# Query weights of heads 2 and 3 placed in two row buffers; expert rows start in the third buffer

## The chip, the cores and the metric

One core of one Trainium2 chip runs the whole kernel. The metric is the device time of one execution in microseconds (us), as the median of several runs.

## The reference, cut to what matters

Two transformer blocks over 256 tokens of width 1024, all in float32. What matters here is the PEER layer at the end of the first block: each token picks 16 of 16384 experts for each of 8 heads, and adds their gated outputs.

```python
def peer(h, w_pq, sub_keys, u_emb, v_emb):
    q = (h @ w_pq).reshape(B, S, PEER_HEADS, 2, PEER_DHALF)          # 8 heads x 2 x 128
    sc = jnp.einsum("bshcd,hcnd->bshcn", q, sub_keys)                # 128 keys per half
    s_top, i_top = lax.top_k(sc, PEER_TOPK)
    cand = s_top[..., 0, :, None] + s_top[..., 1, None, :]           # 16 x 16 candidates
    best, pos = lax.top_k(cand, PEER_TOPK)
    expert_idx = ...                                                 # 16 experts per head and token
    gate = jax.nn.softmax(best, axis=-1)
    # per token: a = gelu(u_emb[expert_idx] . h);  out = sum(gate * a * v_emb[expert_idx])
```

With 128 tokens on the partitions, one "row" of the kernel is one rank of one head for 128 tokens: 128 experts' u and v (1024 + 1024 floats each), fetched from DRAM by index. There are 2 token tiles x 8 heads x 16 ranks = 256 rows of 1 MiB (1.05 MB).

## The kernel before, in words

The kernel is written engine by engine, with hand-placed waits on semaphores; the order of the instructions in each engine's block is the order in which it runs them.

**The weight ring.** All dense weights but one piece come as a stream of chunks of up to 2 MiB (`chunk_list`, L82) through a ring of three slots, loaded by SyncE (L690 to L698). Chunk n goes to slot n mod 3 and waits until the chunk three before it has been used for the last time (`LAST_USE`, L222, or the end of its last part). The order around the change is `attno` 0, 1, `convout` 0, 1, `wout` 0, 1, then the query weights `pq` 0, 1 and 3 (each holds two heads: `pq` 1 is heads 2 and 3), then `va`, `cqkv` 0, `cqkv` 1, `qa`, `ka`. So `pq` 0 waits for `convout` 1, `pq` 1 for `wout` 0, `pq` 3 for `wout` 1, `va` for the last use of `pq` 0 (fill `("pqt", 1, 1)`), `cqkv` 0 for that of `pq` 1 (fill `("pq", 3)`) and `cqkv` 1 for that of `pq` 3 (fill `("pq", 7)`). The weights of heads 4 and 5 (`EARLY_QUERY`, L79) lie elsewhere, loaded in four pieces behind `wout` 0 (L703).

**Fills.** TensorE writes each result into one of six PSUM banks in one fixed order (`fill_list`, L183); `bank_filled` counts them, and other engines wait for a count.

**The start of the expert layer.** TensorE multiplies by `wout`, normalises and turns token tile 0 and computes the first head's query and scores (`first_query_and_scores`, L1138). VectorE selects the first 16 experts in two halves (`first_selection`, L2190, first half signalled at L2218). Then come token tile 1, the queries of heads 0 and 1 (`tile_query`, `tile_scores`) and, on VectorE, the whole selection of head 1 before the first row.

**The row loop**, 256 rows, each passed through four engines:

- GpSimd issues the indirect load of row n (L740 to L753) into row buffer n mod 8 of `gath`, which lies over the first 16384 columns of `pool`, 2048 columns a buffer. Buffers 0 to 3 lie below the split `wout` weights; from row 4 on (`ROWS_BELOW_WEIGHTS`, L167) it first waits for the fill `("wout", 1, 1)`. Row 8 and every 16th row wait for the selection; from row 8 on, row n also waits until row n - 8 has been used by TensorE (`wait_spent`, L624).
- VectorE makes the dot product of the u half with the token (`dot`, L2235, L2242), and between the dots the selection of the head after next (`select_step`).
- ScalarE makes gelu, gate and a 128x128 diagonal, two rows at a time (L1654 to L1671), four diagonals deep.
- TensorE multiplies the diagonal by the v half (two matmuls of 512 columns, L1221) into two PSUM banks of their own.

**Queries inside the row loop.** Heads 2 to 7 have their query (`pq`, 16 accumulated products of 256 columns for both token tiles, L800) and scores (`sc`, L1201) placed ahead of certain rows of TensorE's order by `QUERY_SLOTS` (L163). ScalarE copies each out after the diagonal four rows later (`QUERY_COPY_AFTER`, L166).

After the row loop come the rest of the second block's projections, attentions and feed-forward layers, which the change leaves as they are but for the ring slots that their chunks lie in.

Of the kernel before, what the change touches and what calls it, by code (L numbers as in the profile page):

```python
# [25 lines left out]
D = 1024  # L26
# [50 lines left out]


EARLY_QUERY = 2  # L79


def chunk_list():  # L82
    out = [(("glu", i), 4096) for i in range(4)] + [(("q1", i), 4096) for i in range(2)] + [(("kv1", 0), 2048)]
    out += [(("gate", i), 4096) for i in range(4)]
    out += [(("attno", i), 4096) for i in range(2)] + [(("convout", i), 4096) for i in range(2)]
    out += [(("wout", i), 4096) for i in range(2)]
    out += [(("pq", i), 4096) for i in range(4) if i != EARLY_QUERY]
    out += [(("va", 0), 4096), (("cqkv", 0), 4096), (("cqkv", 1), 4096), (("qa", 0), 4096), (("ka", 0), 4096),
            (("kpe_uq", 0), 3328), (("uq_ukv", 0), 3584), (("evout", 0), 4096), (("evout", 1), 4096)]
    for layer in range(2):  # L90
        if layer:
            out += [(("uz", 0), 4096), (("vz", 0), 4096), (("qd", 0), 4096), (("kd", 0), 4096), (("vd", 0), 4096),
                    (("ws", 0), 1024), (("odout", 0), 4096), (("odout", 1), 4096)]
        out += [(("gu%d" % layer, i), 4096) for i in range(KF // 2)]
        out += [(("down%d" % layer, i), min(4, KF - 4 * i) * D) for i in range(-(-KF // 4))]
    return out
# [61 lines left out]
def fm_fills(name, chunks=1):  # L158
# [1 line left out]

QUERY_SLOTS = {0: ("pq", 2), 2: ("sc", 2), 8: ("pq", 3), 14: ("sc", 3), 19: ("pq", 4), 25: ("sc", 4),  # L163
               30: ("pq", 5), 36: ("sc", 5), 42: ("pq", 6), 48: ("sc", 6), 54: ("pq", 7), 60: ("sc", 7)}
QUERY_LAG = 4
QUERY_COPY_AFTER = {n + (QUERY_LAG if n else 0): fill for n, fill in QUERY_SLOTS.items()}  # L166
ROWS_BELOW_WEIGHTS = 4  # L167
SELECT_FIRST_AT = (7, 8, 9, 10, 11, 12, 13, 14, 15)
TOKEN_CHUNKS = (("va", 0), ("cqkv", 0), ("cqkv", 1))
NORM_SLOT = 15  # L170
# [150 lines left out]
        self.scale, self.table, self.sinks, self.column = scale, table, sinks, column  # L321


def build(nc, stream, early_query, consts, t5const, params, rows, keys_in, late_rows, x_in, positions, t5_in, rpb_in, uv, out):
    with ExitStack() as ctx:
        def sb(name, shape, dt=F32):
            return ctx.enter_context(nc.sbuf_tensor(name, shape, dt))
# [1 line left out]
        def sem(name):  # L329
            return ctx.enter_context(nc.semaphore(name))  # L330
# [113 lines left out]
        qpT = view(att, 5120, 2, 2, S)  # L444
        keys = tab[:, :, :].rearrange("p h j -> p (h j)")[:, 0:2048].rearrange("p (m n) -> p m n", n=NKEYS)
        gath = view(pool, 0, NROWS, 2 * D)
        scores = view(att, 0, NT, 2 * PH * NKEYS)
        cand = att[:, 4096:4096 + TOPK * TOPK]
        first_cand = att[:, 1024:1024 + TOPK * TOPK]
# [57 lines left out]
        row_landed = sem("row_landed")  # L507
        keys_landed = sem("keys_landed")
        early_query_landed = sem("early_query_landed")
        pos_landed = sem("pos_landed")  # L510
        t5_landed = sem("t5_landed")
        rpb_landed = sem("rpb_landed")
# [171 lines left out]
        @block.sync  # L684
        def _(sp):
            for t in range(NT):
                sp.dma_start(x[:, t, :], x_in[P * t:P * t + P, :]).then_inc(x_landed[t], 16)
            sp.dma_start(cst[:, :], consts).then_inc(const_landed, 16)
            sp.dma_start(par[:, :], params).then_inc(param_landed, 16)
            for n, (name, width) in enumerate(CHUNKS):  # L690
                if n >= NSLOT:
                    before = CHUNKS[n - NSLOT][0]
                    if before in LAST_PART:
                        wait_part_used(sp, *LAST_PART[before])
                    else:
                        sp.wait_ge(bank_filled, FILL_NO[last_use(before)] + 1)
                src = stream[CHUNK_AT[n]:CHUNK_AT[n + 1]].rearrange("(p w) -> p w", p=P)
                sp.dma_start(ring[:, n % NSLOT, 0:width], src).then_inc(chunk_landed[n % NSLOT], 16)  # L698
                if name == ("wout", 0):
                    sp.wait_ge(bank_filled, FILL_NO["attno", 1, 1] + 1)  # L700
                    sp.wait_ge(t5_stored, 16)
                    sp.wait_ge(rpb_stored, 16)
                    for c, piece in enumerate(query_pieces):  # L703
                        sp.dma_start(piece, early_query[:, 1024 * c:1024 * c + 1024].rearrange("p (k n) -> p k n", k=2)
                                     ).then_inc(early_query_landed, 16)
            for t in range(NT):
                sp.wait_ge(out_ready, t + 1)
                sp.dma_start(out[P * t:P * t + P, :], xn[:, t, :]).then_inc(out_stored, 16)
            sp.wait_ge(out_stored, 16 * NT)
# [3 lines left out]
        def _(gp):  # L713
# [26 lines left out]
            for n in range(NT * SLOTS):  # L740
                if n == ROWS_BELOW_WEIGHTS:
                    gp.wait_ge(bank_filled, FILL_NO["wout", 1, 1] + 1)
                if n == 0:
                    gp.wait_ge(first_ranks, 1)
                elif n == TOPK // 2:
                    gp.wait_ge(selected, 1)
                elif n % TOPK == 0:
                    gp.wait_ge(selected, n // TOPK + 1)
                if n >= NROWS:
                    wait_spent(gp, n - NROWS)  # L750
                gp.indirect_dma_start(out=gath[:, n % NROWS, :], out_offset=None, in_=uv,  # L751
                                      in_offset=bass.IndirectOffsetOnAxis(ap=experts[:, n:n + 1], axis=0)
                                      ).then_inc(row_landed_in[n % NROWS], 16)  # L753

# [24 lines left out]
        def _(pe):  # L779
# [404 lines left out]
            def query(kind, head):  # L1184
                dst = begin((kind, head))
                if kind == "pq":
                    if head // 2 == EARLY_QUERY:
                        pe.wait_ge(early_query_landed, 16 * len(query_pieces))
                        w = [query_pieces[k // 2][:, k % 2, :] for k in range(KD)]
                    else:  # L1190
                        chunk = wait_chunk(pe, ("pq", head // 2))[:, 0:4096].rearrange("p (k n) -> p k n", k=KD)
                        w = [chunk[:, k, :] for k in range(KD)]
                    for j in range(2):
                        c = 2 * P * (head % 2) + P * j
                        last = accumulate(dst[:, S * j:S * j + S], [(w[k][:, c:c + P], hT[:, k, :]) for k in range(KD)])
                else:
                    wait_emptied(pe, ("pq", head))
                    for t in range(NT):
                        for c in range(2):
                            at = 2 * NKEYS * t + NKEYS * c  # L1200
                            last = nc.tensor.matmul(dst[:, at:at + NKEYS], qpT[:, head % 2, c, tile128(t)],  # L1201
                                                    keys[:, 2 * head + c, :], start=True, stop=True)
                last.then_inc(bank_filled, 1)

            for t in range(NT):
                if t:
                    pe.wait_ge(sums_added, 2 * t)
                for k in range(SLOTS):
                    n = SLOTS * t + k
                    if n in QUERY_SLOTS:  # L1210
                        query(*QUERY_SLOTS[n])
                    if t and k == NORM_SLOT:
                        tile_transposes("mix0", 0, xn[:, 0, :])
                    if t and k in TOKEN_SLOTS:
                        if k == TOKEN_SLOTS[0]:
                            wait_tile("mix0", 0)
                        name, i = TOKEN_CHUNKS[TOKEN_SLOTS.index(k)]
                        token_chunk(name, i, 0)
                    pe.wait_ge(diag_ready, n + 1)
                    for half in range(2):  # L1220
                        last = nc.tensor.matmul(psum[:, RB + half, :], diag[:, n % NDIAG, :],  # L1221
                                                gath[:, n % NROWS, D + 512 * half:D + 512 * half + 512],
                                                start=k == 0, stop=k == SLOTS - 1)
                        if k == SLOTS - 1:
                            last.then_inc(sums_done, 1)
                    if k < SLOTS - 1:
                        last.then_inc(row_spent, 1)
# [512 lines left out]
        def _(dve):  # L1740
# [494 lines left out]
            def dot(n):  # L2235
# [2 lines left out]
                if k == 0 and pair >= 4:  # L2238
                    dve.wait_ge(acts_ready, pair - 3)
                dve.wait_ge(row_landed_in[n % NROWS], 16 * (n // NROWS + 1))  # L2240
                row_u = gath[:, n % NROWS, 0:D]
                ins = V.tensor_tensor_reduce(out=row_u, in0=row_u, in1=xn[:, n // SLOTS, :], scale=1.0,  # L2242
                                             scalar=0.0, op0=ALU.mult, op1=ALU.add,
                                             accum_out=dots[:, pair % 4, k:k + 1])
# [261 lines left out]
```

## Time and profile before

| | us |
|---|---|
| median of 3 runs | 1607.2 |
| lowest, highest | 1601.48, 1609.42 |
| the profiled execution's own time | 1604.03 |
| its span, first to last instruction | 1602.1 |
| busy: TensorE | 1447.7 |
| busy: VectorE | 1017.3 |
| busy: ScalarE | 646.3 |
| busy: GpSimd | 312.3 |
| GpSimd's first and last row issued at | 266.8, 927.7 |

The profile gives the busy time of each engine, the share of the span and rate of the 16 DMA engines, the chain of work that ended last (followed back from the last instruction through what released each step), and every instruction with what ended the idle time before it. TensorE's busy time is modelled and overlaps: its sum in a stretch is no proof that it was at its peak. An issue of a DMA is listed at the time at which the engine gave it out, and not at its landing.

### The profile page before, as it was taken

The page shows a single profiled execution, that of the slowest core. Times are in us where ns is not written, and L with a number is a line of the kernel's source. Part 1 is how long each engine was busy: PE and PEld are TensorE (multiplying, and loading weights), DVE is VectorE, ACT ScalarE, POOL GpSimd, SP SyncE. Part 2 cuts the span into 40 slices and gives each one's busy share as a digit, 9 for nine tenths or more (in the row PEclk, how much of TensorE's full clock was granted, in tenths as well). Part 3 has the DMA queues.
Part 4 walks back from the last instruction along what each step waited for, and adds up shares of the span by engine and source line. Part 5 has one row for each costly group of instructions (what it writes and reads, how often), then busy time and mean ns, then how long its engine had stood idle before and what let it go on. Part 6 is the DMA issues. An engine that isn't in the chain of part 4 may idle for free.

```text
span 1602.1 us, 16913 instructions
## 1 busy us (share of the span) xinstructions
PE 1447.7 (90%) x6102; PEld 1002.6 (63%) x6102; DVE 1017.3 (63%) x1989; ACT 646.3 (40%) x1313; POOL 312.3 (19%) x298
## 2 busy tenths in 40 slices
PE   8998898989977777797987779989999999999998
PEld 6987897745533332333333237767888889878886
DVE  6999976767667777777665543346555455565553
ACT  4423662333333334433333224454444345544442
POOL 2000001144444444434434410400000000000000
PEclk9999999999999999999999999999999999999999
DMA  7546455999999999999999955413454444145451
GB/s 296 205 164 137 121 216 217 395 398 418 412 421 421 419 420 420 420 397 421 411 410 417 421 223 191 148 73 130 185 206 162 182 166 164 73 190 203 165 201 62
DMA packets 52212, 428.59 MB, mean 268 GB/s; under 512 B 6696, under 2 KB 6840, under 8 KB 10144
## 3 DMA queue, kind: packets, MB, share of 16 engines
q0 software_dynamic: 40464, 279.18, 43.7%
q1 hardware_dynamic: 11664, 148.33, 24.4%
q8 instruction: 49, 0.80, 0.2%
q14 instruction: 35, 0.29, 0.0%
HBM read 422.49 MB, written 4.98 MB: 267 GB/s over the span
## 4 chain that ended last, share of the span: by engine, by line
PE 62%; DMA 20%; DVE 10%; ACT 5%; issue 2%; POOL 0%; SPq 0%; DVEq 0%; ACTq 0%; POOLq 0%
DMA pool<-uv,experts 19%; PE psum L933 12%; PE psum L935 12%; PE psum L934 12%; PE psum L800 11%; PE psum L1221 10%; DVE pool L2242 3%; PE psum L834 2%; DVE pool L2010 2%; PE psum L880 1%; DVE ring_lo L1834 1%; ACT diag L1670 1%; ACT xn L1316 1%; DVE att L1811 1%; ACT coef L1664 1%
## 5 line engine op out<-in xcount | busy, mean ns | idle before, releaser
L1221 PE MATMUL psum<-pool,diag 128*128 128x512 f32 x1024 | 482.5, 621 | 109.9 <-ACT diag L1670 109.6
L1221 PEld LDWEIGHTS psum<-pool,diag 128*128 128x128 f32 x1024 | 194.7, 197 | 388.6 <-issue 213.0
L2242 DVE CUSTOM_DVE_ANT_0 pool<-pool,xn 128x1024 f32<-128x1024 f32 x256 | 313.4, 1226 | 195.8 <-DMA pool<-uv,experts 193.8
L751 POOL DMA_INDIRECT pool<-uv,experts x256 | 281.4, 1099 | 514.4 <-PE psum L1221 366.4
L1834 DVE TENSOR_TENSOR ring_lo<-ring,w_hi 128x2048 fp32r<-128x2048 f32 x76 | 174.0, 2292 | 114.0 <-ACT w_hi L1412 113.9
L1660 ACT ACTIVATE acts<-dots 128x2 f32<-128x2 f32 x128 | 26.0, 203 | 366.6 <-DVE dots L2242 366.4
L1412 ACT ACTIVATE w_hi<-ring 128x2048 fp32r<-128x2048 f32 x76 | 144.4, 1908 | 65.1 <-PE psum L935 36.0
L933 PE MATMUL psum<-w_hi,h_hi 128*128 128x512 f32 x400 | 161.2, 403 | 2.5 <-DVE ring_lo L1834 0.9
L934 PE MATMUL psum<-ring_lo,h_hi 128*128 128x512 f32 x400 | 157.2, 393 | 0.0
L935 PE MATMUL psum<-w_hi,h_lo 128*128 128x512 f32 x400 | 156.1, 390 | 0.0
L800 PE MATMUL psum<-hT,ring 128*128 128x256 f32 (+1 forms) x544 | 116.8, 376 | 0.8 <-issue 0.8
L800 PEld LDWEIGHTS psum<-hT,ring 128*128 128x128 f32 x544 | 100.2, 201 | 16.5 <-issue 3.1
L2010 DVE SCALAR_TENSOR_TENSOR pool<-pool,par 128x256 f32<-128x256 f32 x240 | 98.3, 486 | 0.2
L1670 ACT ACTIVATE diag<-cst,coef 128x128 f32<-128x128 f32 x256 | 89.6, 394 | 9.3 <-PE psum L1221 5.0
L933 PEld LDWEIGHTS psum<-w_hi,h_hi 128*128 128x128 f32 x400 | 75.2, 188 | 21.5 <-issue 3.1
L935 PEld LDWEIGHTS psum<-w_hi,h_lo 128*128 128x128 f32 x400 | 75.2, 188 | 18.6
L934 PEld LDWEIGHTS psum<-ring_lo,h_hi 128*128 128x128 f32 x400 | 74.9, 187 | 15.3
L933 PE MATMUL psum<-w_hi,gu_hi 128*128 128x512 f32 x176 | 70.1, 398 | 0.0
L934 PE MATMUL psum<-ring_lo,gu_hi 128*128 128x512 f32 x176 | 69.0, 392 | 0.0
L935 PE MATMUL psum<-w_hi,gu_lo 128*128 128x512 f32 x176 | 68.7, 390 | 0.0
L1664 ACT ACTIVATE coef<-acts,gates 128x1 f32<-128x1 f32 x256 | 61.4, 287 | 4.2
L1312 ACT ACTIVATE pool<-psum 128x512 f32<-128x512 f32 (+1 forms) x47 | 23.1, 505 | 88.7 <-PE psum L800 62.1
(327 smaller groups left out, 2156.1 us busy)
## 6 DMA issues: line engine op xcount, KB each, us to landing
ring<-stream SPq DMA_DIRECT2D x65, 2048.0 KB, 7.7
pool<-uv,experts POOLq DMA_INDIRECT x256, 12.5
ring<-stream SPq DMA_DIRECT2D x3, 1024.0 KB, 4.8
t_scratch<-tab POOLq DMA_DIRECT2D x1, 2048.0 KB, 56.3
rpb_scratch<-tab POOLq DMA_DIRECT2D x1, 1792.0 KB, 23.1
ring<-stream SPq DMA_DIRECT2D x1, 1792.0 KB, 8.1
row<-rows POOLq DMA_DIRECT2D x1, 1672.0 KB, 11.3
ring<-stream SPq DMA_DIRECT2D x1, 1664.0 KB, 6.6
```

The source lines that it names most:

```text
L751: gp.indirect_dma_start(out=gath[:, n % NROWS, :], out_offset=None, in_=uv, in_offset=bass.IndirectOffsetOnAxis(ap=experts[:, n:n + 1], ax ...
L800: last = nc.tensor.matmul(dst, lhsT, rhs, start=(i == 0), stop=(i == len(pairs) - 1))
L933: nc.tensor.matmul(dst, lhsT[0], rhs[0], start=start, stop=False)
L934: nc.tensor.matmul(dst, lhsT[0], rhs[1], start=False, stop=False)
L935: return nc.tensor.matmul(dst, lhsT[1], rhs[0], start=False, stop=stop)
L1221: last = nc.tensor.matmul(psum[:, RB + half, :], diag[:, n % NDIAG, :], gath[:, n % NROWS, D + 512 * half:D + 512 * half + 512], start=k = ...
L1412: nc.scalar.activation(part_high(layer, q), part_raw(layer, q), ACT.Copy).then_inc(hi_split, 1)
L1664: ins = nc.scalar.activation(coef[:, b, j:j + 1], acts[:, b, j:j + 1], ACT.Copy, scale=gates[:, n:n + 1])
L1670: nc.scalar.activation(diag[:, n % NDIAG, :], ident, ACT.Copy, scale=coef[:, b, j:j + 1]).then_inc(diag_ready, 1)
L1834: V.tensor_tensor(part_low(layer, q), part_raw(layer, q), part_high(layer, q).bitcast(F32), ALU.subtract).then_inc(lo_split, 1)
L2010: ins = V.scalar_tensor_tensor(y[:, m, :], src, tap, y[:, m, :], ALU.mult, ALU.add)
L2242: ins = V.tensor_tensor_reduce(out=row_u, in0=row_u, in1=xn[:, n // SLOTS, :], scale=1.0, scalar=0.0, op0=ALU.mult, op1=ALU.add, accum_out ...
```

## The change

The 2 MiB of `pq` 1 leave the stream and become an input of their own, `row_query`. SyncE loads them right behind `pq` 0 into the first two row buffers (`pool` columns 0 to 4095, `row_weights`), behind a wait for the fill `("convout", 1, 1)`, which is the last reader of what lay there. Row n of the loop goes into row buffer (n + 2) mod 8, so rows 0 to 5 go into buffers 2 to 7 and rows 6 and 7 into buffers 0 and 1. Row 2 (not row 4) is the first to wait for `("wout", 1, 1)`. Row 6 gets a new wait on GpSimd, for the fill `("pq", 3)`. The query of head 3 moves from row 8 to row 1 of TensorE's order, and ScalarE's copy of it from row 12 to row 5. In the ring, `pq` 3 now waits for `wout` 0, `va` for `wout` 1, `cqkv` 0 for the last use of `pq` 0, and `cqkv` 1 for the fill `("pq", 7)`, as before.

```diff
+ROW_QUERY = 1
...
-    out += [(("pq", i), 4096) for i in range(4) if i != EARLY_QUERY]
+    out += [(("pq", i), 4096) for i in range(4) if i not in (EARLY_QUERY, ROW_QUERY)]
...
-QUERY_SLOTS = {0: ("pq", 2), 2: ("sc", 2), 8: ("pq", 3), 14: ("sc", 3), 19: ("pq", 4), 25: ("sc", 4),
+QUERY_SLOTS = {0: ("pq", 2), 1: ("pq", 3), 2: ("sc", 2), 14: ("sc", 3), 19: ("pq", 4), 25: ("sc", 4),
...
-ROWS_BELOW_WEIGHTS = 4
+ROWS_BELOW_WEIGHTS = 2
...
+        row_weights = pool[:, 0:2 * 2 * D]
...
+                if name == ("pq", 0):
+                    sp.wait_ge(bank_filled, FILL_NO["convout", 1, 1] + 1)
+                    sp.dma_start(row_weights, row_query).then_inc(row_query_landed, 16)
...
+                if n == NROWS - 2:
+                    gp.wait_ge(bank_filled, FILL_NO["pq", 2 * ROW_QUERY + 1] + 1)
                 if n >= NROWS:
                     wait_spent(gp, n - NROWS)
-                gp.indirect_dma_start(out=gath[:, n % NROWS, :], out_offset=None, in_=uv,
+                gp.indirect_dma_start(out=gath[:, (n + 2) % NROWS, :], out_offset=None, in_=uv,
...
+                    elif head // 2 == ROW_QUERY:
+                        pe.wait_ge(row_query_landed, 16)
+                        w = [row_weights[:, 512 * k:512 * k + 512] for k in range(KD)]
...
-                                                gath[:, n % NROWS, D + 512 * half:D + 512 * half + 512],
+                                                gath[:, (n + 2) % NROWS, D + 512 * half:D + 512 * half + 512],
...
-                row_u = gath[:, n % NROWS, 0:D]
+                row_u = gath[:, (n + 2) % NROWS, 0:D]
```

## Rows read from the trace of the kernel before

**Rows 1.** The page: share and rate of the DMA engines in 40 slices of 40 us

```profile
DMA  7546455999999999999999955413454444145451
GB/s 296 205 164 137 121 216 217 395 398 418 412 421 421 419 420 420 420 397 421 411 410 417 421 223 191 148 73 130 185 206 162 182 166 164 73 190 203 165 201 62
```

**Rows 2.** The chain that ended last: start, us, engine and line

```profile
254.71 2.92 PE psum L1145 x24
...
289.36 6.91 PE psum L800 x32
296.27 3.43 PE psum L1221 x8
299.70 0.89 PE psum L1201 x8
300.59 10.30 PE psum L1221 x24
310.90 6.91 PE psum L800 x32
...
321.61 11.03 DMA pool<-uv,experts
```

**Rows 3.** Table by stretch: us, busy of PE, PEld, DVE, ACT, POOL, PEclk, DMA share, GB/s

```profile
247.00:262.00 15.00, 14.23 (x82) 11.63 (x82) 6.41 (x24) 3.75 (x11) 0.00 (x0) 1.00 0.00 1
263.00:298.50 35.50, 30.81 (x176) 26.86 (x175) 27.98 (x87) 9.94 (x26) 7.91 (x8) 0.90 1.00 407
298.50:308.00 9.50, 9.50 (x29) 4.69 (x28) 4.11 (x13) 3.17 (x10) 4.96 (x6) 1.00 0.86 306
308.00:345.00 37.00, 32.89 (x95) 18.06 (x94) 23.39 (x58) 13.15 (x40) 14.71 (x14) 0.91 1.01 422
350.00:355.00 5.00, 5.00 (x16) 2.70 (x15) 4.17 (x14) 0.92 (x3) 0.98 (x2) 1.00 0.90 352
355.00:360.00 5.00, 5.00 (x13) 2.24 (x12) 4.46 (x15) 1.49 (x5) 3.29 (x3) 1.00 0.88 311
450.00:640.00 190.00, 144.03 (x297) 57.19 (x296) 137.10 (x348) 69.24 (x206) 81.47 (x75) 0.95 1.01 420
```

**Rows 4.** SyncE's issues of ring chunks, in order of time: start, us

```profile
239.14 0.33 SPq L698 DMA_DIRECT2D ring<-stream  x1
...
262.41 0.33 SPq L698 DMA_DIRECT2D ring<-stream  x1
...
267.98 0.33 SPq L698 DMA_DIRECT2D ring<-stream  x1
...
288.21 0.33 SPq L698 DMA_DIRECT2D ring<-stream  x1
...
317.83 0.33 SPq L698 DMA_DIRECT2D ring<-stream  x1
```

**Rows 5.** The chunk issued at 239.14: its size and us to landing

```profile
ring<-stream SPq DMA_DIRECT2D x1, 2048.0 KB, 7.8
```

**Rows 6.** GpSimd's issues in order of time: rows 0, 7 and 8

```profile
266.79 1.06 POOL L751 DMA_INDIRECT pool<-uv,experts  x1 [133.96 <-DVE experts L2218]
...
275.69 1.14 POOL L751 DMA_INDIRECT pool<-uv,experts  x1 [0.30 <-issue]
298.76 0.94 POOL L751 DMA_INDIRECT pool<-uv,experts  x1 [21.94 <-PE psum L1221]
```

**Rows 7.** VectorE's dots in order of time: rows 16 and 23

```profile
330.29 1.23 DVE L2242 CUSTOM_DVE_ANT_0 pool<-pool,xn 128x1024 f32<-128x1024 f32 x1 [4.44 <-DMA pool<-uv,experts]
...
347.62 1.22 DVE L2242 CUSTOM_DVE_ANT_0 pool<-pool,xn 128x1024 f32<-128x1024 f32 x1 [1.15 <-DMA pool<-uv,experts]
```

**Rows 8.** TensorE in order of time, behind its idle time ahead of row 16

```profile
336.54 7.81 PE L1221 MATMUL psum<-pool,diag 128*128 128x512 f32 x12 [4.11 <-ACT diag L1670]
```

**Rows 9.** Table by stretch, columns as in Rows 3: the stretch with the queries

```profile
296.00:439.00 143.00, 136.21 (x419) 76.70 (x418) 97.77 (x256) 51.12 (x156) 61.17 (x54) 0.98 0.99 404
```

More of the change, by code:

```diff
@@ L321, in __init__, with build @@
         self.scale, self.table, self.sinks, self.column = scale, table, sinks, column
-def build(nc, stream, early_query, consts, t5const, params, rows, keys_in, late_rows, x_in, positions, t5_in, rpb_in, uv, out):
+def build(nc, stream, early_query, row_query, consts, t5const, params, rows, keys_in, late_rows, x_in, positions, t5_in, rpb_in, uv, out):
     with ExitStack() as ctx:
@@ L509, in build @@
         early_query_landed = sem("early_query_landed")
+        row_query_landed = sem("row_query_landed")
         pos_landed = sem("pos_landed")
@@ L2494 @@
     arrays = {
-        "stream": stream, "early_query": parts["pq", EARLY_QUERY], "consts": consts, "t5const": t5, "params": params, "rows": rows, "late_rows": late,
+        "stream": stream, "early_query": parts["pq", EARLY_QUERY], "row_query": parts["pq", ROW_QUERY],
+        "consts": consts, "t5const": t5, "params": params, "rows": rows, "late_rows": late,
         "x_in": a["x"].reshape(S, D), "positions": a["positions"].reshape(NT, P).T, "t5_in": a["t5_bias_2"],
```

## The prediction

> **What bounds the kernel now.** I read the page's strip of DMA activity first, then the chain that ended last, then the tables by stretch, and last the single issues. The strip [rows 1] shows one long plateau near 420 GB/s: the row loop, in which 256 MiB of expert rows come in. The chain [rows 2] tells what a change at its start can reach: it runs along TensorE (queries and row products) up to 319.5 us and then hangs on a DMA of a row, and it comes back to such DMAs to the loop's end. The table [rows 3] says it without a chain: no byte moves from 247 to 262 us, 407 GB/s from 263 to 298.5, only 306 from 298.5 to 308, then 422 and 420. So from 263 us on the DMA engines set the pace, and the time of the loop is (bytes of the plateau) / (about 422 GB/s) plus the holes. Two rules follow: a MiB taken out of the plateau is worth what it took, and a hole costs its length. The one hole that the change touches is the one near 300 us.
>
> The price of a MiB: the dots of rows 16 and 23 both waited for a landing [rows 7], so seven rows took 347.62 - 330.29 = 17.33 us, 2.48 us a row (1.05 MB, 423 GB/s). I call 1 MiB one unit.
>
> **Part 1, a load leaves the plateau.** Ring chunks are issued at 239.14 (`pq` 0), 262.41 (`pq` 1), 267.98 (`pq` 3), 288.21 (`va`) and 317.83 (`cqkv` 0) [rows 4]. After the change every chunk behind `pq` 0 takes the place of the one ahead: `pq` 3 at 262.4, `va` at 268.0, `cqkv` 0 at 288.2. The heads 2 and 3 weights are issued right behind `pq` 0 at about 239.5, as both wait for the same fill. `pq` 0 took 7.8 us to land [rows 5], so at 246.9; two more units behind it take 2 x 2.48 us and land at 252, in the stretch in which nothing moves [rows 3]. The first query needs `pq` 0 at 254.71 [rows 2], so even if the two loads shared the engines evenly it would not be late. SyncE's added wait is already met, and nothing is due behind it before 262. Two units leave the plateau: 2 x 2.48 = **-5.0 us**.
>
> Here a page speaks against my price. The trace moves 420 to 423 GB/s over hundreds of us [rows 3, 7]. The Trainium skill, page "DMA: Bandwidth & Descriptors", section Specifications, gives one core a limit of about 358 GB/s from its memory; by that estimate the two units would be worth 2.1 MB / 358 GB/s = 5.9 us, and the sum below one microsecond less. The measured rate decides, and the sum goes by it.
>
> **Part 2, row 6 waits for head 3's query.** Before, GpSimd gave out rows 0 to 7 from 266.79 to 275.69, and row 8 at 298.76, as soon as row 0 was spent [rows 6]. Counting units from 263 us: `pq` 1, `pq` 3, `va` and eight rows are 14 units, and 35.5 us x 407 GB/s = 14.4 MB says that they were through at 298.5 [rows 3]; 2.54 us a unit. After, only rows 0 to 5 can go: `pq` 3, `va`, `cqkv` 0 and six rows are 12 units, through at 263 + 12 x 2.54 = **293.5 us**. Then the engines stand idle until row 6.
>
> When does row 6 go? TensorE starts head 2's query at 289.36 and ends it at 296.27; nothing ahead of that is changed, so it stands. Row 0 takes half of the 3.43 us of two rows, 1.72 us, to 297.99. Now head 3's query comes, 6.91 us as the one at 310.90 [rows 2]: filled at **304.90**. GpSimd issued row 8 at 298.76, 0.77 us after row 0's end at 297.99 [rows 2, 6]; the same lag puts row 6 at **305.7**. Rows 7, 8 and 9 are queued behind it on GpSimd, which does nothing else.
>
> The restart has a price too. Before, the 9.5 us from 298.5 at 306 GB/s hold 9.5 x (1 - 306/422) = 2.6 us of nothing [rows 3]: as if full rate had begun at 301.1, 2.3 us behind the issue at 298.76. After: 305.7 + 2.3 = **308.0**.
>
> **The sum.** At its restart (301.1) the kernel before had left 248 rows and `cqkv` 0 and 1, 252 units. The changed one at its restart (308.0) has left 250 rows and `cqkv` 1, 252 units as well. So the loop ends 308.0 - 301.1 = **6.9 us later**; or: the hole grows from 2.6 to 14.5 us, +11.9, and the moved load gives back 5.0.
>
> **Part 3, what costs nothing, and its cover.** Head 3's query itself is moved, not added; behind row 1 it no longer stands at row 8, and TensorE works off rows 1 to 5 (five times 1.72 us and the 0.89 us of scores, done at about 314.4) while row 6 lands. The copy on ScalarE after row 5 waits for nothing late. The scores of head 2 are copied only after row 7's diagonal, some 11 us later than before, so VectorE's selection of head 2 starts about 11 us later; it is due when row 32 is issued, and row 16 comes only near 336 us, so rows at 2.48 us hide it. Row 2's earlier wait is met: `wout` (1, 1) is filled when SyncE issues its chunk at 267.98, and GpSimd comes to row 2 two steps of (275.69 - 266.79) / 7 = 1.27 us behind row 0, at 269.3 [rows 6]. The later ring slots change in number only. If VectorE's cover failed, the price would be another hole, case D.
>
> **Unknown, with both ends.** The restart lag: row 6 restarts an empty queue, and rows 6 to 9 can be issued back to back, where rows 10 on waited for TensorE; so it may cost nothing; or, with more engines starting from nothing, twice the 2.3 us. I take 2.3, from the one restart that the trace has. The hole at 350 to 360 us (352 and 311 GB/s, 5 x (1 - 352/422) + 5 x (1 - 311/422) = 2.1 us [rows 3]) comes with head 4's query at row 19; everything there is pushed along, so I leave it, with ends of nothing and twice its size: -2.1 to +2.1. Together with the lag's -2.3 to +2.3: +2.5 to +11.3.
>
> The sum is made against the profiled execution, 1604.03 us by its own clock, 3.2 us under the median of 1607.2. 1604.0 + 6.9 = 1610.9; against the median, **1614**. A measurement of this kernel can tell about 0.5%, 8 us, from no change, so the forecast lies just inside.
>
> **Rivals.**
>
> A, the backlog covers the wait: were the transfers slower or more than I count, the idle hole would vanish and only the -5.0 would stay, 1602. It needs row 6 issued before the queue runs dry, at 293.5 by my count and not at 305.7; break-even (a restart at 301.1) needs it at 298.8. For it: DMA share 1.00 up to 298.5. Against: that backlog held four units that the changed kernel doesn't have in it (two rows and `pq` 1), and 16 products stand ahead of the issue.
>
> B, TensorE sets the end of this stretch: it is busy 136 of 143 us between 296 and 439 [rows 9], and the change gives it the same work in another order. Then the loop is as long as before: 1607. Against it: the chain leaves TensorE at 319.5 for a landing [rows 2], and TensorE stood idle 4.11 us ahead of row 16 [rows 8].
>
> C, more is lost than the hole, the slower side: after the hole rows arrive one by one instead of in a backlog, TensorE runs dry between them and its clock falls. The trace has such a place: after 4.11 us of idling, three rows took 7.81 us, 2.6 us a row, where two took 3.43 at full clock [rows 2, 8]. If head 4's query at row 19 met TensorE in that state it could take twice its 6.91 us. The point from which it decides is the depth of rows in flight: eight rows are 19.8 us, and if spent-to-landed plus the query exceed that, the excess is a new hole of up to 6.9 us: 1621. Against: from 450 to 640 us the mean clock is 0.95 and the DMA rate still 420 [rows 3]. The Trainium skill, page "TensorE: Matmul & The Clock Gate", Part 1, has the same rule, that an idle TensorE falls back to half its clock; a full halving of that query is what this rival prices.
>
> D, the change does not do what it says: the extra load delays `pq` 0 or lands late. It would need 7.8 us of landing to become more than 15.6 (254.71 - 239.14). Then each us over it is a us on TensorE's chain: 1616 and up. Or the late selection of head 2 opens a hole of its own, of like size.
>
> **How the numbers follow.** Forecast 0.60, A 0.05, B 0.12, C 0.18, D 0.05. The forecast's own ends are +2.5 and +11.3, 1610 to 1618. The range given reaches from B, less 2 us for the scatter of a median, to C: 1605 to 1621. Slower by over 0.5% (over 1615.2): C and D but for their mildest (0.17) and a quarter of the forecast (0.15), 0.32. Faster by over 0.5% (under 1599.2): a tail of A, 0.03. Within: 0.65.
>
> **What the changed profile would show.** Five ring-side loads at 239.1, 239.5, 262.4, 268.0 and 288.2, none near 318 to 325. GpSimd: six issues from 266.8, then one at about 305.7 released by L800. DMA rate near zero from about 294 to 307, then 420. TensorE: two blocks of L800 with one row between them, ending near 304.9. Last row issued near 927.7 + 6.9 = 934.6. The prediction is wrong if the hole is under 8 us, if the rate behind it stays under 415, or if the rows' end moves by something other than hole less 5.0.

## The result, and the profile after

| | before | after |
|---|---|---|
| median of 20 runs, us | 1604.36 | 1610.15 |
| lowest, highest | 1601.48, 1610.02 | 1607.74, 1613.75 |
| the profiled execution's own time | 1604.03 | 1610.49 |
| its span | 1602.1 | 1608.6 |
| row 0 issued at | 266.79 | 265.87 |
| the load behind the last row (L756, now L764) issued at | 928.65 | 933.41 |
| from the one to the other, "the loop" | 661.86 | 667.54 |
| row 48 issued at, behind the stretch that the change touches | 401.15 | 404.64 |

The changed kernel is slower: ratio 1.003 with a 95% interval of 1.002 to 1.0039, which is +4.8 us (3.2 to 6.3) of 1604.4. In the two profiled executions the loop is 5.7 us longer, and the span 6.5. All times in us. Up to row 48 the loop is 4.4 us longer (134.36 before, 138.77 after, counted from row 0's issue); the other 1.3 us lie behind it, where the change has the same loads and the same order.

The table by stretch of the changed kernel, with the columns of [rows 3]:

```profile
247.00:262.00 15.00, 14.23 (x83) 11.65 (x82) 7.22 (x26) 2.92 (x9) 0.00 (x0) 1.00 0.19 79
263.00:293.00 30.00, 25.31 (x156) 23.06 (x155) 24.57 (x78) 7.90 (x18) 5.83 (x6) 0.89 0.98 399
293.00:305.50 12.50, 12.50 (x51) 9.53 (x51) 1.33 (x4) 2.83 (x10) 0.94 (x1) 1.00 0.08 33
305.50:345.00 39.50, 32.95 (x79) 14.38 (x78) 26.09 (x68) 12.61 (x37) 21.42 (x18) 0.91 0.99 404
350.00:355.00 5.00, 5.00 (x24) 4.34 (x23) 2.22 (x3) 1.18 (x4) 0.00 (x0) 1.00 1.01 415
355.00:360.00 5.00, 5.00 (x13) 2.22 (x12) 4.65 (x21) 1.97 (x6) 1.89 (x2) 1.00 1.01 416
450.00:640.00 190.00, 148.01 (x301) 59.50 (x301) 132.28 (x341) 65.30 (x202) 81.29 (x74) 0.91 1.01 418
```

Against [rows 3] the reader sees three things. The stretch before 262 us now moves bytes: the load that left the loop. From 293 to 305.5 there is the forecast hole (a stretch in which the DMA engines move little or nothing), 33 GB/s, while TensorE is busy all the time. And the second, small hole of 350 to 360 us (352 and 311 GB/s before) is gone.

GpSimd's issues in order of time, rows 5 to 7:

```profile
272.28 0.94 POOL L759 DMA_INDIRECT pool<-uv,experts  x1 [0.30 <-issue]
304.26 0.94 POOL L759 DMA_INDIRECT pool<-uv,experts  x1 [31.04 <-PE psum L808]
305.51 0.94 POOL L759 DMA_INDIRECT pool<-uv,experts  x1 [0.30 <-issue]
```

Row 6 waited 31.04 us and was released by the query (L808), where before row 8 was released by a row's product [rows 6]. TensorE in order of time shows what it waited for: head 2's query, row 0, head 3's query, row 1.

```profile
288.30 7.07 PE L808 MATMUL psum<-hT,pool 128*128 128x256 f32 x32
295.20 1.88 PE L1232 MATMUL psum<-pool,diag 128*128 128x512 f32 x4
296.92 7.07 PE L808 MATMUL psum<-hT,pool 128*128 128x256 f32 x32
303.83 1.88 PE L1232 MATMUL psum<-pool,diag 128*128 128x512 f32 x4
```

The DMA issues by line, between 225 and 262 us, give the moved load's size and time to landing. Issued at 238.60, it was there at 250.9, ahead of the first query:

```profile
pool<-row_query SPq DMA_DIRECT2D x1, 2048.0 KB, 12.3
```

### The profile page after: what moved, and what is told of

The parts are those of the page before. It is cut to its first block, busy times and chain, and to the rows that moved or that the text cites. A ratio compares the mean times of both kernels' runs of the same rounds, so it can differ in the third digit from the quotient of the medians.

```text
span 1608.6 us, 16913 instructions
## 1 busy us (share of the span) xinstructions
PE 1452.3 (90%) x6102; PEld 1003.7 (62%) x6102; DVE 1016.4 (63%) x1989; ACT 646.3 (40%) x1313; POOL 324.0 (20%) x298
## 4 chain that ended last, share of the span: by engine, by line
PE 57%; DMA 21%; DVE 12%; ACT 5%; issue 4%; POOL 1%; SPq 0%; DVEq 0%; ACTq 0%; POOLq 0%
DMA pool<-uv,experts 20%; PE psum L941 12%; PE psum L942 12%; PE psum L943 12%; PE psum L1232 9%; PE psum L808 8%; DVE pool L2253 3%; PE psum L842 2%; DVE pool L2021 2%; PE psum L888 1%; DVE ring_lo L1845 1%; POOL pool L759 1%; ACT diag L1681 1%; ACT xn L1327 1%; ACT coef L1675 1%
## 5 line engine op out<-in xcount | busy, mean ns | idle before, releaser
L1232 PE MATMUL psum<-pool,diag 128*128 128x512 f32 x1024 | 487.0, 626 | 111.5 <-ACT diag L1681 111.3
L1232 PEld LDWEIGHTS psum<-pool,diag 128*128 128x128 f32 x1024 | 195.4, 198 | 394.2 <-issue 214.5
L759 POOL DMA_INDIRECT pool<-uv,experts x256 | 292.9, 1144 | 507.9 <-PE psum L1232 326.8
L808 PE MATMUL psum<-hT,ring 128*128 128x256 f32 (+1 forms) x480 | 102.1, 374 | 0.8 <-DVE hT L2155 0.8
L808 PEld LDWEIGHTS psum<-hT,ring 128*128 128x128 f32 x480 | 87.8, 202 | 14.0 <-issue 2.7
## 6 DMA issues: line engine op xcount, KB each, us to landing
pool<-uv,experts POOLq DMA_INDIRECT x256, 12.5
pool<-row_query SPq DMA_DIRECT2D x1, 2048.0 KB, 12.3
```

The source lines that it names most:

```text
L759: gp.indirect_dma_start(out=gath[:, (n + 2) % NROWS, :], out_offset=None, in_=uv, in_offset=bass.IndirectOffsetOnAxis(ap=experts[:, n:n + ...
L808: last = nc.tensor.matmul(dst, lhsT, rhs, start=(i == 0), stop=(i == len(pairs) - 1))
```

## The experiments

The theory is the prediction's count, called the counting theory: the DMA engines set the pace, the loop ends at (time at which full rate begins) plus (units then left), so a hole costs its length and a unit 2.5 us. The rival is that TensorE, in one order or another, sets the end. Every kernel was timed, with 5 to 12 runs, against the kernel before on the same chip; the intervals are at 95%. Each has one profile, and its loop carries what that one execution lost or gained elsewhere.

### One half of the change at a time

**x1, the load leaves, no hole** (kernel before):

```diff
-    out += [(("pq", i), 4096) for i in range(4) if i != EARLY_QUERY]
+    out += [(("pq", i), 4096) for i in range(4) if i not in (EARLY_QUERY, 1)]
...
-                    if head // 2 == EARLY_QUERY:
+                    if head // 2 in (EARLY_QUERY, 1):
```

> The kernel before without the 2 MiB of the weights of heads 2 and 3: their queries use the weights of heads 4 and 5 that lie ready, so two units leave the loop and nothing waits for a row buffer. (It leaves out the true weights of heads 2 and 3, so other experts are fetched.) Counting theory: 14 units still stand ahead of row 8's issue (cqkv 0 takes the place of pq 1 ahead of it), the same small hole follows, two units fewer are left: -5.0 us, 1599.4 against 1604.4, ratio 0.997. Rival, TensorE sets the end of the stretch from 296 to 439 us: its work is the same, so 0, ratio 1.000.

Measured 0.9968 (0.9957 to 0.9979), -5.1 us; the loop of its profile is 656.99, 4.9 shorter. The size is the counting theory's, and the rival is out: TensorE's work was the same and the time fell. But the profile shows that more than the load moved. Behind head 4's query the loss of the kernel before is nearly gone (416 GB/s for 372, see the second hole below), and the 22 us from about 359.1 on, around head 5's query, have one that the kernel before has not in its place (422 GB/s from 366.2 to 388.2):

```profile
359.10:381.10 22.00, 21.53 (x67) 12.29 (x66) 17.25 (x48) 9.86 (x28) 9.48 (x8) 1.00 0.99 395
```

So -5.1 is the sum of the load and of small holes that moved, and not the load's price alone.

**x2, the hole, no load leaves** (kernel before):

```diff
-QUERY_SLOTS = {0: ("pq", 2), 2: ("sc", 2), 8: ("pq", 3), 14:
+QUERY_SLOTS = {0: ("pq", 2), 1: ("pq", 3), 2: ("sc", 2), 14:
...
+                if n == NROWS - 2:
+                    gp.wait_ge(bank_filled, FILL_NO["pq", 3] + 1)
```

> The kernel before with head 3's query at row 1 and the new wait of row 6 on it, but all weights in the ring as before: the hole alone, without the load moved. Counting theory: 12 units are through at about 293.5, full rate again from about 308.0 with 254 units left against 252 at 301.1: +6.9 + 5.0 = +11.9 us, 1616.3, ratio 1.0074. By what the changed kernel measured (+4.8) plus the load's 5.0 it would be +9.8, ratio 1.006. Rival, TensorE sets the end: the same work in another order, 0 us.

Measured 1.0044 (1.0028 to 1.0059), +7.1 us (4.5 to 9.5): clearly slower, yet less than both numbers. Its profiled loop, 671.77, is 9.9 longer. Its table by stretch has the hole, and near the place of the second one hardly any loss (the second line is the 22 us from the start of head 4's query, and [rows 3] has 352 and 311 GB/s in the same place of the kernel before):

```profile
293.50:305.50 12.00, 12.00 (x52) 9.66 (x51) 2.03 (x4) 3.10 (x11) 0.00 (x0) 1.00 0.15 61
352.70:374.70 22.00, 21.98 (x74) 13.17 (x73) 17.23 (x49) 6.10 (x21) 10.23 (x9) 1.00 1.00 408
```

So 11.9 was too much, in part by the second hole that went away. Up to row 48 the profile's loop is 9.1 us longer, 0.8 lie behind it; the runs' 7.1 is 2 us less, with 9.1 still inside its interval. The two halves measured one by one give -5.1 + 7.1 = +2.0, and the whole change +4.8. With intervals of about 2 us on either half this is no proof of a term of its own, and none is shown.

**x3, head 3's query at row 1, no wait, no load moved** (kernel before): the first hunk of x2 alone.

> The kernel before with head 3's query at row 1 instead of row 8, and nothing else: no new wait, no load moved. Counting theory: row 8 is issued at 298.8 as before, but row 9 needs row 1, which now stands behind the query and ends at 306.6, so full rate comes back at about 308 with 247 rows and two chunks, 251 units, left: 308.0 - 301.1 less one unit of 2.5, +4.4 us, ratio 1.0027. Were the added wait the whole cause of the hole, this would be 0. Rival, TensorE sets the end: 0.

Measured 1.0013 (1.0001 to 1.0025), +2.1 us; loop 664.15, +2.3. Slower without any new wait: the query itself, standing ahead of row 1, keeps row 9 from being issued (at 307.31, for 300.01 in the kernel before). The size was again 2 us under the forecast, and the interval all but touches zero.

### The length of the hole

**x4, the query at row 5** (changed kernel):

```diff
-QUERY_SLOTS = {0: ("pq", 2), 1: ("pq", 3), 2: ("sc", 2), 14:
+QUERY_SLOTS = {0: ("pq", 2), 2: ("sc", 2), 5: ("pq", 3), 14:
```

> The changed kernel with head 3's query ahead of row 5 instead of row 1. The query then ends after four more rows of 1.72 us and the scores' 0.89, so row 6 is issued 7.8 us later, about 312 us. Counting theory, a hole costs its length: 7.8 us more than the changed kernel, ratio to before 1.003 + 0.0049 = 1.008. If the backlog or later slack took up part of a hole, clearly less than 7.8; if TensorE set the end, the same as the changed kernel, 1.003.

Measured 1.0078 (1.0061 to 1.0095), +12.5 us; loop 675.11, 7.6 more than the changed kernel's. Row 6 went out at 313.22, counted from row 0's issue 8.5 us later than in the changed kernel. Some 8 us more of hole cost 7.7 us.

**x5, both queries ahead of row 0** (changed kernel):

```diff
+                    if n == 0:
+                        query("pq", 2)
+                        query("pq", 3)
-                    if n in QUERY_SLOTS:
+                    elif n > 1 and n in QUERY_SLOTS:
                         query(*QUERY_SLOTS[n])
```

> The changed kernel with both queries ahead of row 0: head 3's no longer waits behind row 0's two matmuls, so row 6 is issued one row, 1.72 us, earlier. Counting theory: the hole is 1.7 us shorter and nothing else moves, +3.1 against the kernel before, ratio 1.0019. If row 0's later end (row 8 waits for it) made a hole of its own, nothing is gained: 1.003.

Measured 1.0022 (1.0012 to 1.0032), +3.5; loop 666.02, 1.5 less than the changed kernel's. It agrees with -1.7, but the intervals of the two overlap.

**x6, one head a row buffer** (changed kernel; the host lays the weights out head by head):

```diff
-                        w = [row_weights[:, 512 * k:512 * k + 512] for k in range(KD)]
+                        at = 2 * D * (head % 2)
+                        w = [row_weights[:, at + 256 * k:at + 256 * k + 256] for k in range(KD)]
...
-                if n == NROWS - 2:
-                    gp.wait_ge(bank_filled, FILL_NO["pq", 2 * ROW_QUERY + 1] + 1)
+                if NROWS - 2 <= n < NROWS:
+                    gp.wait_ge(bank_filled, FILL_NO["pq", 2 * ROW_QUERY + n - NROWS + 2] + 1)
```

> The changed kernel with head 2's weights in the first row buffer and head 3's in the second, so that row 6 waits for head 2's query only and is issued at about 296.8, and only row 7 waits for head 3's. Counting theory: one unit more is through in the hole, 2.5 us less than the changed kernel: +2.3 against before, ratio 1.0014. If what counts is when the flow of rows starts again (row 7 on, unchanged at 304.3), and not how many units are left, nothing is gained: 1.003.

Measured 1.0022 (1.0011 to 1.0032), +3.5, halfway between the two theories' 2.3 and 4.8. Row 6 did go out in the hole, at 298.69; the second hole stood in its profile (below), which takes back what was left. That profile is of the slowest of its 12 runs (1612.93, median 1608.0), so it says little of the kernel's size.

**x9, a faster TensorE ahead of the queries.** The profile gave a lever of another kind: TensorE had idled 3.35 us ahead of the turning of token tile 1, and ran the queries behind it at 0.58 of its clock from 276 to 284 us. The edit, on the changed kernel (the 7 are matmuls whose result nobody reads, issued into the gap; called a warming below):

```diff
-            tile_transposes("N2", 1, xn[:, 1, :])
+            tile_transposes("N2", 1, xn[:, 1, :], 7)
```

> The changed kernel with seven matmuls of 128x256 ahead of the turning of token tile 1, where TensorE stood idle 3.35 us; the four tile queries behind it ran at a granted clock of 0.5 to 0.66 and took 9.95 us, where two heads of them at full clock are 2 x 3.57 us. The queries of heads 2 and 3 follow directly, so row 6 should be issued 2.8 us earlier. Counting theory: a hole shorter by 2.8 us is a loop shorter by 2.8 us: +2.0 against before, ratio 1.0013. If the hole's length did not count us for us: 1.003.

Measured 1.0015 (1.0006 to 1.0024), +2.4, 2.4 less than the changed kernel. The table from 276 to 284 us, first of the changed kernel, then of x9:

```profile
276.00:284.00 8.00, 7.17 (x40) 6.80 (x39) 7.48 (x32) 0.26 (x1) 0.00 (x0) 0.58 1.01 419
```

```profile
276.00:284.00 8.00, 6.68 (x55) 6.02 (x54) 6.87 (x25) 1.57 (x3) 0.00 (x0) 1.00 1.00 419
```

and TensorE of x9 in order of time, turning and tile queries:

```profile
277.24 1.09 PE L842 MATMUL psum<-cst,xn 128*128 128x128 f32 x8 [0.33 <-DVE xn L2152]
279.32 7.38 PE L808 MATMUL psum<-hT,ring 128*128 128x128 f32 x64 [0.99 <-DVE hT L2155]
```

The clock stays at its upper level and the tile queries take 7.38 instead of 9.95; the loop of its profile is 3.9 shorter, 3.1 of them up to row 48. The intervals of x9 and of the changed kernel overlap (1.0006 to 1.0024, and 1.0020 to 1.0039). With x4 this makes two edits of different kinds, one that lengthens the hole and one that shortens it, each paid about us for us; x4 shows it clearly, x9 less so.

### The second hole

The 22 us from the start of head 4's query (row 19) show it best. First the kernel before, then the changed one:

```profile
344.20:366.20 22.00, 22.00 (x75) 13.28 (x74) 16.59 (x47) 5.95 (x20) 9.06 (x10) 1.00 0.95 372
```

```profile
347.80:369.80 22.00, 22.00 (x74) 13.16 (x73) 17.44 (x49) 6.11 (x21) 9.72 (x9) 1.00 1.01 406
```

At 421 GB/s for a full queue, these are losses of 22 x (1 - 372/421) = 2.6 us and 0.8 us. What TensorE did for rows 16 to 18 right before that query is, before, the row in [rows 8], 7.81 us behind 4.11 of idling, and in the changed kernel

```profile
342.34 5.63 PE L1232 MATMUL psum<-pool,diag 128*128 128x512 f32 x12 [1.29 <-ACT diag L1681]
```

Over the kernels, with the time from the start of row 16's dot to that of head 4's query, and with the loss in the 22 us after those, which head 5's query falls into:

| kernel | rows 16 to 18 | idle ahead of row 16 | row 16's dot to the query | loss in the 22 us | in the next 22 us |
|---|---|---|---|---|---|
| before | 7.81 | 4.11 | 13.9 | 2.6 | 0.0 |
| x3 | 7.11 | 3.05 | 13.1 | 1.5 | 0.0 |
| x6 | 7.12 | 2.42 | 13.1 | 1.8 | 0.0 |
| after | 5.63 | 1.29 | 11.7 | 0.8 | 0.0 |
| x1 | 5.63 | 0.81 | 12.3 | 0.3 | 1.3 |
| x4 | 5.64 | 1.01 | 11.5 | 0.2 | 1.1 |
| x5 | 5.64 | 0.96 | 11.6 | 0.6 | 0.0 |
| x8 | 5.63 | 0.85, behind eight matmuls | 11.7 | 0.6 | 0.2 |
| x10 | 5.31 | none, behind eight matmuls | 13.7 | 2.9 | 0.0 |
| x12 | 5.62 | 2.63 | 11.7 | 1.5 | 0.0 |

The longer TensorE takes from row 16's arrival to the query, the larger the loss, with x12 as the exception (x8, x10 and x12 are told below). In x1 and x4 part of the loss has only moved on by one query.

**x8** asks whether that is a cause (kernel before; the bank is the one that head 4's query then fills):

```diff
+                    if n == TOPK:
+                        warmed = begin_warm(("pq", 4), WARM_ROWS)    # WARM_ROWS = 8
```

> The kernel before with eight matmuls of 128x256 into a free bank ahead of row 16, where TensorE stood idle for 4.11 us and its granted clock was at half for the next rows. In the profiles so far the granted clock of 335 to 345 us and the DMA hole of 350 to 360 us go together: 0.68 and 0.83 with the hole, 1.00 four times without. If the half clock makes the hole, this kernel shows clock 1.00 there, over 410 GB/s from 350 to 360, and a loop shorter by the hole's 2 us: ratio 0.9987. If the two only stand beside each other, the hole stays with the clock up: 1.000. If the extra matmuls themselves delay row 16, slower: 1.001.

Measured 0.9985 (0.9973 to 0.9996), -2.4 us. Its clock from 335 to 345 us, and its 22 us:

```profile
335.00:345.00 10.00, 9.15 (x30) 5.21 (x29) 4.94 (x8) 4.53 (x17) 3.75 (x3) 1.00 1.02 420
341.90:363.90 22.00, 22.00 (x74) 13.16 (x73) 17.24 (x49) 6.11 (x21) 10.20 (x9) 1.00 1.01 409
```

Rows 16 to 18 in TensorE's order:

```profile
336.45 5.63 PE L1224 MATMUL psum<-pool,diag 128*128 128x512 f32 x12 [0.85 <-ACT diag L1673]
```

They took 5.63 us, head 4's query began 2.0 us earlier, counted from row 0's issue, and the loss fell from 2.6 to 0.6 us. The whole loop of this profile is only 0.3 us shorter, 661.57: up to row 48 it gains 1.7 us, and behind it this execution took 1.5 more. The timed runs say -2.4 (0.6 to 4.3). So in the kernel before the low clock is how TensorE comes late, and most of this hole goes with it. The changed kernel loses less there too, and its TensorE had work left nearly up to row 16; that the one comes of the other is inferred, not shown.

### A version that beats both

**x7, the two queries first** (x6, and the following; the hunks that move the queries of heads 0 and 1 for the second token tile and their copies are left out here):

```diff
+            query("pq", 2)
+            query("pq", 3)
             for t in range(NT):
...
-QUERY_SLOTS = {0: ("pq", 2), 1: ("pq", 3), 2: ("sc", 2), 14: ("sc", 3),
+QUERY_SLOTS = {2: ("sc", 2), 6: ("pqt", 0, 1), 8: ("sc", 3), 12: ("pqt", 1, 1), 13: ("sct", 0, 1), 18: ("sct", 1, 1),
```

> As x6, and the queries of heads 2 and 3 are computed ahead of those of heads 0 and 1 for the second token tile (which are not needed before the second half of the rows and go to rows 6 and 12, their scores to rows 13 and 18, head 3's scores to row 8). Head 2's query then ends at about 285.4 and head 3's at 292.3: row 6 is issued at 285.9, row 7 at 292.8 and row 8 behind row 0 at about 296. Counting theory: 11 units are through at 291, full rate again from about 295.1 with 253 units left against 252 at 301.1: -3.5 us, 1600.9, ratio 0.9978; up to 2 us better without the hole near 355. If the two queries of 4.9 us at rows 6 and 12 open a hole of their own, about 0 or slower: 1.000 to 1.002.

Measured 1.0001 (0.999 to 1.0012): nothing, a miss by 3.5 us. Its issues of rows 6 and 7:

```profile
287.53 1.93 POOL L759 DMA_INDIRECT pool<-uv,experts  x1 [14.16 <-PE psum L808]
294.44 1.90 POOL L759 DMA_INDIRECT pool<-uv,experts  x1 [4.98 <-PE psum L808]
```

Row 7 went out 1.6 us later than counted, since both queries now stood where the clock is low (16.79 us for 13.8), and rows 16 to 18 were no longer three in a row, with a loss of 1.3 us at head 4's query. I had taken both durations at full clock. That accounts for some 2 of the 3.5 us: up to row 48 its profile is 1.3 us shorter than that of the kernel before, and behind it 2.0 longer.

**x10, both warmings on the kernel before** (x8 and the hunk of x9).

> The kernel before with both warmings: seven matmuls ahead of the turning of token tile 1 and eight ahead of row 16. Counting theory: head 2's query ends 2.6 us earlier, row 8 is issued as soon as row 0's diagonal and product allow, about 296.2, just ahead of the end of the backlog at 298.5, so the first hole of 2.6 us goes as well as the second of 2.1: -4.7 us, 1599.8, ratio 0.9971. If only the second counts, as in x8: 0.9985.

Measured 0.9981 (0.9967 to 0.9994), -3.1. Its first hole is gone, its second is not, though the clock is up:

```profile
293.50:310.00 16.50, 16.50 (x51) 8.82 (x50) 9.32 (x23) 7.10 (x23) 7.63 (x7) 1.00 1.01 420
335.00:345.00 10.00, 10.00 (x33) 6.00 (x32) 4.94 (x8) 4.59 (x13) 4.77 (x4) 1.00 1.01 417
344.90:366.90 22.00, 22.00 (x75) 13.28 (x74) 16.62 (x47) 6.09 (x21) 8.46 (x10) 1.00 0.92 366
```

That corrects the reading of x8: the clock is one way in which TensorE comes late to row 16. Here rows 14 and 15 came late, the eight matmuls of the warming ran from 336.28 on and held TensorE until 339.7, with row 16's diagonal ready at 337.3. From row 16's dot to head 4's query it took 13.7 us at full clock, as long as the kernel before with its low one, and the loss is as large.

**x12, the first warming alone** (kernel before, the one line of x9).

> The kernel before with only the seven matmuls ahead of the turning of token tile 1 (x10 without the eight ahead of row 16). In x10's trace row 16's diagonal was ready at 337.3 us, but the eight matmuls held TensorE until 339.7, four rows were in flight when head 4's query began, and the second hole stood there at 315 and 300 GB/s. If those matmuls had come in the way, this kernel has the first hole gone and the second no larger than before's: -2.6 to -4.7 us, ratio 0.9984 to 0.9971, at least as good as x10. If it was the clock that they should have kept up, the second hole grows and this is slower than x10: 0.999.

Measured 0.9981 (0.9971 to 0.9992), -3.1, as good as x10 without the eight matmuls. Its table:

```profile
293.50:310.00 16.50, 16.50 (x52) 8.99 (x52) 9.35 (x28) 4.39 (x16) 8.69 (x8) 1.00 1.00 412
340.00:362.00 22.00, 22.00 (x75) 13.28 (x74) 17.89 (x49) 6.10 (x21) 8.88 (x10) 1.00 0.98 392
```

412 GB/s where the kernel before had its first hole, and a second of 1.5 us. One line on the kernel before gives 3 us.

**x11, x7 with both warmings** (seven matmuls, and six ahead of row 14).

> x7 with both warmings (six matmuls ahead of row 14, where that kernel's TensorE stood idle). In x7 the queries of heads 2 and 3 took 16.79 us instead of 13.8 at the low clock, and a hole of 1.2 us stood at 350 to 355. Counting theory: row 7 is issued 3.0 us earlier and the second hole is gone: 4.2 us less than x7, -4.0 against before, ratio 0.9975. If the two tile queries at rows 6 and 12 hold the rows up instead, no more than 1 us less than x7: 0.9995.

Measured 0.9975 (0.9965 to 0.9985), -4.0 us, median 1600.7 beside 1604.8 of the kernel before: the fastest of the study that computes everything, by a little. It keeps the change's idea, weights in row buffers, and gives the buffers back in time: rows 6 and 7 went out at 285.54 and 292.44. Whether it beats x12 can't be said; their intervals overlap.

### Two parts of the loop

The profiles can be cut where row 48 is issued, behind both holes:

| kernel | row 0 to row 48, against before | row 48 to the last row | timed runs, against before |
|---|---|---|---|
| before | 0 | 526.6 | 0 |
| after | +4.4 | 527.8 | +4.8 |
| x1 | -4.7 | 526.3 | -5.1 |
| x2 | +9.1 | 527.4 | +7.1 |
| x3 | +1.4 | 527.4 | +2.1 |
| x4 | +13.6 | 526.2 | +12.5 |
| x5 | +3.5 | 527.2 | +3.5 |
| x6 | +3.1 | 527.9 | +3.5 |
| x7 | -1.3 | 528.5 | +0.2 |
| x8 | -1.7 | 528.0 | -2.4 |
| x9 | +1.3 | 527.0 | +2.4 |
| x10 | -2.2 | 526.7 | -3.1 |
| x11 | -4.1 | 527.3 | -4.0 |
| x12 | -3.0 | 527.9 | -3.1 |

Both parts are counted between issues on GpSimd; row 48's is, in the kernel before and in the changed one,

```profile
401.15 1.80 POOL L751 DMA_INDIRECT pool<-uv,experts  x1 [2.93 <-PE psum L1221]
```

```profile
404.64 1.80 POOL L759 DMA_INDIRECT pool<-uv,experts  x1 [2.94 <-PE psum L1232]
```
The second part has the same loads in every kernel and differs by up to 2.3 us from one profile to the next, and the kernel before has one of the shortest. What the whole loop of a single profile shows against it is therefore good to about 2 us; the first part lies nearer to the timed runs for most kernels, and x2 is off by 2.0.

## Why the prediction was right or wrong

**The bound: right.** A load taken out of the plateau gave 5.1 us (x1) where two rows' price is 5.0, small holes that moved included; a longer hole cost its length (x4), a shorter one gave it back (x9).

**By the page's rate the load would have been worth 5.9 us.** The Trainium skill, page "DMA: Bandwidth & Descriptors", section Specifications, has the limit of about 358 GB/s; every profile here moved 404 to 423 GB/s for tens of us, and x1's interval (3.4 to 6.9 us) holds both prices.

**Part 1: right.** The load landed at 250.9, where I had 252; the chunks behind it were issued at 261.49, 267.09 and 287.30, 0.9 us ahead of the places named, as row 0 was.

**Part 2, the hole: right in place and length.** Row 6 was due at 305.7 and went out at 304.26 in an execution that ran 0.92 us ahead at row 0, so 305.2 on the old scale. From 305.5 to 345 us, 404 GB/s of 422 is a loss of 39.5 x (1 - 404/422) = 1.7 us, so full rate as if from 307.2, 308.1 on the old scale; predicted 308.0. Part of that closeness is luck: row 6 went out 0.5 us sooner than counted, and the lag behind it was 2.9 us where I took 2.3.

**The first step that failed: "A measurement of this kernel can tell about 0.5%, 8 us, from no change, so the forecast lies just inside".** With it a sum of +6.9 became a forecast of no change that can be told, 0.65 for "within" and 0.32 for slower by more. The 8 us are as large as the spread of the three single runs that stood behind it (1601.48 to 1609.42). With twenty runs a side the interval is 1.5 us to each side, and +4.8 (3.2 to 6.3) is clearly slower; "slower, by 5 to 7 us" is what the sum said.

**The second is a term of the sum, under "Unknown": "everything there is pushed along, so I leave it".** The hole behind head 4's query was not pushed along; of its 2.6 us, 0.8 were left, a term of -1.8 that I had at 0 (my ends for it, -2.1 to +2.1, hold it). +6.9 - 1.8 = +5.1, and +4.8 was measured, +4.4 in the profile up to row 48. I had seen the row that tells of it, 4.11 us of idling and three rows in 7.81 [rows 8], and had used it for rivals B and C only, in C as something that the change might bring. It was something that the kernel before had, and that the change took away: after it, rows 6 to 15 came later and kept TensorE at work until shortly before row 16; it idled 1.29 us there and took 5.63. This chain is read from one profile of each kernel. x8 takes the low clock away by a separate edit of the kernel before, and the timed runs put that at 2.4 us (0.6 to 4.3).

**The base was off too.** 1607.2 was the middle of three runs; over twenty the kernel before has 1604.36. The forecast of 1614 stands 3.9 us over the measured 1610.15, 2.8 of them from the base and 2.1 from the sum, less 1.0 between the ratio and the medians.

**The rivals.** A, the backlog covers the wait: no, 33 GB/s from 293 to 305.5 us. B, TensorE sets the end: no, by x1 and x4; that it was busy 136 of 143 us [rows 9] did not make it the bound. It counts here through the holes, by when it gives a row buffer back (x9, x12). C, the low clock makes it worse: the low clock ahead of head 4's query is real, but stands in the kernel before, so the change gained by it. The Trainium skill's rule on an idle TensorE (page "TensorE: Matmul & The Clock Gate", Part 1) agrees with the traces: granted clock 0.58 behind 3.35 us of idling, 1.00 behind 0.33. D: no, the load was in time, and the later selection of head 2 held nothing up: row 32 went out at 365.95 released by a row's product (L1232), as before the change.

**Left open.** Why x2 measured 7.1 where its profile has 9.1 up to row 48, x3's 2.1 where 4.4 less some 1.1 of second hole was due, x12's loss of 1.5 us with TensorE in time, and why a small hole moves on to head 5's query in x1 and x4. The loss of the second hole is read from one profile a kernel; x8 alone confirms its size in timed runs. A kernel in which the weights leave the row buffers without any TensorE query (a copy to another place) was not tried.

## What to carry to other kernels

In a stage that is paced by DMA, count what is in the queue when the next issue is held, and from when on it can be issued: moving a load ahead of the stage is worth its transfer, but a borrowed buffer that comes back late costs the whole gap, and here about 5 us gained (x1) stood against 7.1 lost when measured alone (x2), or 9.8 by the whole change (4.8 and the 5.0 of the load). Before a hole is called fixed, see what TensorE does just before it: here a few idle us mostly went with a lower clock, the next products came late, and the queue behind them ran dry; such a hole moves with a change upstream, as from head 4's query to head 5's in x1. And before one profile is held against another, see how much they differ where the kernels are the same, here by up to 2.3 us. The cheap repair may stand on the critical chain far ahead, as here seven idle-time matmuls that made four small queries 2.6 us shorter.

## What the runs showed of the hardware that was not expected

Small idle times ahead of TensorE work were dearer than they looked: with 4.11, 3.05 and 2.42 us of idling ahead of row 16 three rows took 7.1 to 7.8 us, with 0.81 to 1.29 and once 2.63 (x12) they took 5.6. Idling alone does not decide, then, and what else does was not tried. And an empty queue of row loads does not start at full rate: it was as if full rate began 2.3 us (before) and 2.9 us (after) behind the first issue, an estimate from the rates of 306 and 404 GB/s in the stretches behind it.
